# The 512-token FFN's gate and up projections: from ordinary tiles to seven block products

## The reference, cut to what matters

```
D_MODEL = 1024;  SEQ = 512;  CTX_LEN = 256;  D_FF = 2816     # 22 tiles of 128
def swiglu(h, w1, w2):
    gate, up = jnp.split(h @ w1, 2, axis=-1)
    return (jax.nn.silu(gate) * up) @ w2
def ffn_sublayer(h, m, sub, g_pre, g_post, w1, w2):
    shift, scale, gate = mods_of(m, sub)
    y = swiglu(modulate(rms_norm(h, g_pre[sub]), shift, scale), w1, w2)
    return h + MACARON_WEIGHT * gate * rms_norm(y, g_post[sub])
```

## Time and profile before

| | us |
|---|---|
| median of three timed runs | 3765.51 |
| the profiled execution | 3757.21 |
| its span, first to last instruction | 3755.4 |
| PE busy in the span | 3530.5 (94%) |
| DVE, ACT, POOL busy | 2183.8, 1434.2, 721.5 |
| 512-token FFN: first matmul of its first pair | starts at 2427.65 |
| 512-token FFN: last matmul of its output | ends at 2798.92 |

### The profile page before, as it was taken

How to read it: one execution, slowest core, us unless ns; L and a number is a source line. 1 busy time by engine, 2 the same in 40 slices (tenths; PEclk the granted TensorE clock), 3 DMA queues, 4 the chain that set the end, 5 groups by cost and what they waited for, 6 DMA issues and landing times.

```text
span 3755.4 us, 52062 instructions
## 1 busy us (share of the span) xinstructions
PE 3530.5 (94%) x19855; PEld 3030.4 (81%) x19855; DVE 2183.8 (58%) x3395; ACT 1434.2 (38%) x2510; POOL 721.5 (19%) x299
## 2 busy tenths in 40 slices
PE   6899999988999999999999898899998999899998
PEld 4899997856789999789999676788878898589656
DVE  6888875167488888788887429421226462541134
ACT  4433333157353333543334317432234423221353
POOL 1111112200211111211111220244442232034202
PEclk9999999999999999999999998999998999799899
DMA  6333332110233332433333220123332222022101
GB/s 227 107 124 123 124 120 86 62 36 1 91 118 116 121 117 97 157 109 116 113 113 119 82 70 17 46 90 100 96 95 68 62 79 68 1 73 90 62 1 56
DMA packets 94531, 333.55 MB, mean 89 GB/s; under 512 B 12272, under 2 KB 14576, under 8 KB 93424
## 3 DMA queue, kind: packets, MB, share of 16 engines
q1 hardware_dynamic: 91248, 316.28, 25.5%
q10 hardware_dynamic: 3072, 14.40, 1.0%
HBM read 322.12 MB, written 8.52 MB: 88 GB/s over the span
## 4 chain that ended last, share of the span: by engine, by line
PE 60%; issue 23%; POOL 6%; DVE 6%; ACT 3%; DMA 2%; SPq 0%; POOLq 0%; DVEq 0%; ACTq 0%
PE psum L2348 21%; PE psum L2227 14%; PE psum L2207 13%; POOL w_parts L668 6%; PE psum L2652 1%; PE psum L2668 1%; PE psum L2262 1%; PE psum L2677 1%; PE psum L2450 1%; PE psum L2121 1%; DMA mod_ring<-modw_dram 1%; PE psum L2424 1%; DVE normed L1302 1%; PE psum L2556 1%; DVE mod_products L1390 0%
## 5 line engine op out<-in xcount | busy, mean ns | idle before, releaser
L668 POOL TENSOR_TENSOR w_parts<-w_raw,w_parts 128x1024 fp32r<-128x1024 f32 x289 | 702.5, 2432 | 2929.2 <-ACT w_parts L708 2916.8
L2207 PE MATMUL psum<-h_parts,w_parts 128*128 128x264 f32 (+1 forms) x5712 | 958.2, 330 | 46.8 <-issue 11.8
L2207 PEld LDWEIGHTS psum<-h_parts,w_parts 128*128 128x128 f32 x5712 | 855.4, 191 | 144.4 <-issue 44.6
L708 ACT ACTIVATE w_parts<-w_raw 128x1024 fp32r<-128x1024 f32 x283 | 300.1, 1061 | 1123.7 <-PE psum L2207 722.5
L2227 PE MATMUL psum<-w_parts,hidden_parts 128*128 128x512 f32 x2904 | 668.3, 391 | 16.5 <-DVE hidden_parts L1262 9.6
L2227 PEld LDWEIGHTS psum<-w_parts,hidden_parts 128*128 128x128 f32 x2904 | 544.6, 188 | 135.6 <-issue 14.6
L2348 PE MATMUL psum<-h_parts,w_parts 128*128 128x384 f32 x2880 | 531.6, 336 | 16.4 <-ACT y_tok L855 14.1
L2348 PEld LDWEIGHTS psum<-h_parts,w_parts 128*128 128x128 f32 x2880 | 505.4, 189 | 20.0 <-issue 17.0
L874 ACT ACTIVATE w_parts<-psum 128x512 fp32r<-128x512 f32 x240 | 143.7, 599 | 367.9 <-PE psum L2348 147.9
L2348 PE MATMUL psum<-h_sums,w_parts 128*128 128x384 f32 x1440 | 268.9, 334 | 0.0
L2348 PEld LDWEIGHTS psum<-h_sums,w_parts 128*128 128x128 f32 x1440 | 251.3, 188 | 0.0
(11 more groups left out here) (352 smaller groups left out, 4121.1 us busy)
## 6 DMA issues: line engine op xcount, KB each, us to landing
w_raw<-wu_dram SPq DMA_DIRECT2D x295, 512.0 KB, 3.6
mod_ring<-modw_dram SPq DMA_DIRECT2D x128, 512.0 KB, 4.4
w_raw_pairs<-wg_dram SPq DMA_DIRECT2D x120, 512.0 KB, 3.7
kept_dram<-resid SPq DMA_DIRECT2D x2, 3136.0 KB, 9.9
resid<-kept_dram SPq DMA_DIRECT2D x16, 392.0 KB, 5.8
na_bias<-rpb_dram ACTq DMA_DIRECT2D x6, 896.0 KB, 4.7
four_dft<-four_dram ACTq DMA_DIRECT2D x2, 2048.0 KB, 8.1
mod_first_k<-modw_dram SPq DMA_DIRECT2D x7, 512.0 KB, 10.0
```

The lines of the kernel that those rows point to most:

```text
L668: pool.tensor_tensor(SPL[:, s % 2, 1], RAW[:, s % 2], SPL[:, s % 2, 0].bitcast(F32), ALU.subtract).then_inc(w_split, 1)
L708: act.activation(SPL[:, u % 2, 0], RAW[:, u % 2], ACT.Copy).then_inc(w_hi, 1)
L2207: ins = pe.matmul(PS[:, pair, PSO[a]:PSO[a] + z - a], w[:, wp, k], src[:, xp, k, t0 + a:t0 + z], start=k == 0 and n_ == 0, stop=k == KT - ...
```

## The change

The 512-token FFN becomes the fourth fast FFN. All code of the fast FFN that had 384 columns for half the tokens takes that number from the FFN (`half_tokens`), so the products here are 256 columns wide. The new FFN has no modulation tiles to make beside its work (`MOD_PLAN` is zero there). Its pure weight blocks get their low part from GpSimd (`run_lows`), not from DVE. The weights are stored on the host in the other order.

```
-    fast = [... if sub["kind"] == "ffn" and sub["T"] == T1]
+    fast = [... if sub["kind"] == "ffn"]
...
+            def run_lows(g):                                              # GpSimd
+                for n, (m, p) in enumerate(ORDER):
+                    if m in PURE:
+                        pool.wait_ge(block_hi, PRODUCTS * g + n + 1)
+                        pool.tensor_tensor(w_block(n, 1), raw_half(g, p, *PURE[m]), w_block(n, 0).bitcast(F32),
+                                           ALU.subtract).then_inc(block_low_pure, 1)
...
                 low_parts(start + 4, 4)
                 u = start + 8
                 for g in range(RUNS):
+                    if sub["T"] == SEQ:
+                        run_lows(RUNS * sub["fo"] + g)
                     low_parts(u, 4)
...
             def w_step(g, q):                                             # DVE
-                if q + 3 < PRODUCTS:
+                if q + 3 < PRODUCTS and (half_tokens(g // RUNS) == T1 // 2 or ORDER[q + 3][0] in SUM_BANK):
...
-                        pe.wait_ge(bank_read, yb - T1 // P + to + 1)
+                        pe.wait_ge(bank_read, yb - tiles + min(to + 1, tiles))
...
-                            ins = pe.matmul(bank(to, HT), w_block(n, wp)[:, k], moving(m, xp)[:, k], ...
+                            ins = pe.matmul(bank(to, ht), w_block(n, wp)[:, k], moving(m, xp, ht)[:, k], ...
```

More of the change, by code:

```diff
@@ L377, in build @@
     n = dict(u=0, silu=PRIME, pr=PRIME, e=PRIME, q=0, sq=PRIME, xr=PRIME, att=0, out=0, tr=0, mix=0, eh=0, ph=0, yb=6, bd=0, ys=0, yt=0)
-    fast = [idx for idx, sub in enumerate(subs) if sub["kind"] == "ffn" and sub["T"] == T1]
+    fast = [idx for idx, sub in enumerate(subs) if sub["kind"] == "ffn"]
     for idx, sub in enumerate(subs):
@@ L462, in build, with half_tokens, quarter, normed @@
     assert mod_first_of(1) == 64 and mod_first_of(2) >= MOD_TILES + MOD_FIRST and mod_first_of(3) == DEPTH * MOD_TILES
-    HT = T1 // 2
-    def quarter(i, j, x):
-        return H[:, x, 4 * i:4 * i + 4, HT * j:HT * j + HT]
-    def normed(i, j):
-        return VB[:, 4 * i:4 * i + 4, HT * j:HT * j + HT]
-    def moving(m, x):
-        return {1: quarter(0, 0, x), 2: quarter(1, 0, x), 3: quarter(1, 1, x), 4: quarter(0, 1, x),
-                5: X12[:, 0, x], 6: X12[:, 1, x], 7: X3[:, x]}[m]
+    def half_tokens(fo):
+        return subs[fast[fo]]["T"] // 2
+    def quarter(i, j, x, ht):
+        return H[:, x, 4 * i:4 * i + 4, ht * j:ht * j + ht]
+    def normed(i, j, ht):
+        return VB[:, 4 * i:4 * i + 4, ht * j:ht * j + ht]
+    def moving(m, x, ht):
+        return {1: quarter(0, 0, x, ht), 2: quarter(1, 0, x, ht), 3: quarter(1, 1, x, ht), 4: quarter(0, 1, x, ht),
+                5: X12[:, 0, x, :, 0:ht], 6: X12[:, 1, x, :, 0:ht], 7: X3[:, x, :, 0:ht]}[m]
     def w_block(n, x):
@@ L657, in _ @@
                     u += S_UNITS
-                elif idx == 1:
+                elif sub["kind"] == "mix":
                     w_loads(u, 24)
@@ L857, in fast_run @@
             def fast_run(g, u, sub):
[L859 removed]
+                base, ht = PRODUCTS * g, half_tokens(g // RUNS)
                 def block_high(n):
@@ L880, in kept @@
                         act.wait_ge(signal, free)
-                    act.activation(dst[:], bank(c_bank(p, "Q"), HT), ACT.Copy).then_inc(kept_ready, 1)
+                    act.activation(dst[:, 0:ht], bank(c_bank(p, "Q"), ht), ACT.Copy).then_inc(kept_ready, 1)
                 for q in range(-3, PRODUCTS + 4):
@@ L901, in fast_run @@
                             act.wait_ge(product_done, base + q)
-                            act.activation(TS[:, 0, HT:T1], bank(c_bank(p, "Q"), HT), ACT.Silu).then_inc(silu12_ready, 1)
+                            act.activation(TS[:, 0, ht:2 * ht], bank(c_bank(p, "Q"), ht), ACT.Silu).then_inc(silu12_ready, 1)
                     for p in range(RUN):
@@ L2322, in fast_run @@
             def fast_run(g, fo, yb):
+                ht, tiles = half_tokens(fo), subs[fast[fo]]["T"] // P
                 for n, (m, p) in enumerate(ORDER):
@@ L2347, in fast_run @@
                         for n_, (wp, xp) in enumerate(((0, 0), (0, 1), (1, 0))):
-                            ins = pe.matmul(bank(to, HT), w_block(n, wp)[:, k], moving(m, xp)[:, k], start=m in (1, 7, 2) and k == 0 and n_ == 0,
+                            ins = pe.matmul(bank(to, ht), w_block(n, wp)[:, k], moving(m, xp, ht)[:, k], start=m in (1, 7, 2) and k == 0 and n_ == 0,
                                             stop=k == 3 and n_ == 2, skip_group_check=True)
@@ L2852, in ffn @@
         gate, up = units_of(w1[:, :F_TILES * P]), units_of(w1[:, F_TILES * P:])
-        if (l, s) != (DEPTH - 1, 1):
-            us.extend([gate[0:2], up[0:2]])
-            us.extend(out_units_of(w2[f0 * P:(f0 + nf) * P], 2) for f0, nf in S_PARTS)
-            pairs.append(np.stack([gate[2:], up[2:]], 1))
-            return
-        for f0, nf in F_PARTS:
-            for f in range(f0, f0 + nf, 2):
-                us.extend([gate[f:f + 2], up[f:f + 2]])
-            us.append(out_units_of(w2[f0 * P:(f0 + nf) * P]))
+        us.extend([gate[0:2], up[0:2]])
+        us.extend(out_units_of(w2[f0 * P:(f0 + nf) * P], 2) for f0, nf in S_PARTS)
+        pairs.append(np.stack([gate[2:], up[2:]], 1))
     for l in range(DEPTH):
```

64 lines of the change are left out of this document (32 added, 32 removed).

## The result

The changed kernel takes 3770.62 us (median of 12 runs, 3764.47 to 3779.85) against 3760.98 us of the kernel before (12 runs, 3757.33 to 3771.49). The ratio is 1.0027 (95% interval 1.0019 to 1.0035): some 10 us slower. That is clear of the noise, since the interval lies above 1, but inside the 0.3% that I had called no change, and inside the forecast's own range of 3756 to 3777. From its first matmul to its last output matmul the 512-token FFN takes 381.4 us instead of 371.3, so the whole difference is in it (one profiled execution of each kernel).

What follows compares the result with a forecast made beforehand. TensorE, busy 94% of the span, was taken as the bound: 34.3 + 12.0 + 1.7 + 201.6 + 109.2 + 9.0 + 4.5 = 372.3 us against 371.3, +1.0, so a median of 3766, range 3756 to 3777.

Steps and rivals of the forecast that it cites:

- TensorE's work: Matmuls of the five runs: 0.120 us each, products lasting 1.44 us, 201.6 in all, 16.8 less than before.
- Ahead of the first run: FFN's start: 34.3 us of TensorE work, 12.0 idle (2.3 + 5.0 + 4.7) and 1.7 for a clock fall.
- GpSimd's 128x512 low part: Pure block's low part on GpSimd inside a run: taken as 1.25 us, near half of the 128x1024 one's 2.38.
- The 14th product: Inside a run: the third pair's late weights and the chain to ACT's copy make TensorE wait 0.67 us.
- The 21st product: Inside a run: by the same count of late weights, the fourth pair waits 0.95 us.
- The 7th product: Inside a run: by the same count of late weights, the second pair waits 0.2 us.
- The run's end: First output unit's low part behind GpSimd's last pure block: 0.9 us wait a run, 4.5 in all.
- The tail: FFN's end: as before; eight residual loads of 5.8 us each, covered by the last output part's 21.8 us.
- GpSimd shuts DVE out: Slower rival inside runs: GpSimd blocks DVE's two-SBUF-input instructions, DVE becomes the bound, +14 us, 3780 to 3785; chance 0.17.
- The clock inside the runs: Rival: waits inside runs pull the clock to 1.2 GHz, 1.7 us lost twice a run, +17, 3783; chance 0.04.
- the faster one: Rival: slots free earlier, GpSimd's low parts hidden, no wait inside runs or at their ends, -13.5 us, 3753; chance 0.17.

Runs made afterwards that it cites:

- e1: The changed kernel with the pure blocks' low parts moved back from GpSimd to DVE: 512-token FFN 385.9 us, ratio 1.0032 to the kernel before.
- e2: The changed kernel with GpSimd writing zeros instead of subtracting, so pure blocks' low parts are left out: 512-token FFN 371.9 us, timed once.
- e3: The changed kernel with a fourth slot for pair weights instead of three: 512-token FFN 369.6 us, ratio 0.9990 to the kernel before.
- e5: e3 with the hidden tile's high and low part one step later for a run's first three pairs: 512-token FFN 365.5 us, timed once.
- e10: e9 with the pure blocks' low parts on DVE instead of GpSimd: 512-token FFN 361.6 us, ratio 0.9958 to the kernel before.
- e9: e5 plus the first output unit's high part at step 25, its low part after the last pure block: FFN 359.8 us, ratio 0.9965 to before.
- e11: e9 on the change's three pair slots instead of four: 512-token FFN 376.5 us, ratio 0.9992 to the kernel before.

## Why the prediction held, and where it was off

It was right in its side and within its own range: no change beyond 0.3%. That 3770.6 lies so near the forecast's 3766 is in part luck. The forecast stood on a median of 3765.51 for the kernel before; over twelve runs it was 3760.98. The forecast change was +1.0 us and the measured one is 9.6, so the FFN was missed by 9 us, and "no measurable change" held because 9.6 is still under 11.3.

- *TensorE's work.* Right: products 1.44 us apart.
- *Ahead of the first run.* Right in sum, 46.1 for 48.0, by terms that were off both ways: the idle time inside the first pair was 0.8 (2.3 forecast), the wait for the hidden tile was 3.99 (5.0 forecast), the gaps behind it 0.64 + 0.44 + 1.27 = 2.35 (4.7), the clock fell behind the 3.99 and not ahead of the first product, with 1.9 us lost in 24 matmuls (1.7), and TensorE's own work is the rest, 37.0 (34.3).
- *GpSimd's 128x512 low part.* Right: 1.29 where undisturbed, 1.33 on average, for 1.25.
- *The 14th product.* The chain was right link by link, the size was not: 1.5 to 1.7 instead of 0.67. The step that failed is the time at which the slot comes free, which I had put at 2.1 behind the 7th product; it came 1.5 later. Two things were left out of it. In the list of DVE instructions with both inputs in SBUF I counted "two products, one split" and left out the two sums that read two halves of a pair slot: the sum for product 5, put at 0.61, took 0.93 on average and up to 1.58. And ACT makes the high part of a sum block first, 0.6. e1 shows that the wait stays, at 1.04 to 1.78, when GpSimd holds nothing ahead of it; e2, without any low parts of pure blocks, leaves about half of it; a fourth slot takes all of it (e3).
- *The 21st product.* 0.63 to 0.72 in four runs and 2.03 in the last, for 0.95. The reason given, the same chain of late weights, is wrong for the four: a fourth slot leaves them at 0.63 (e3), and the place of the hidden tile's high part on ACT makes them (e5). It holds for the last, where the load took 4.82 us.
- *The 24th product.* Not forecast: 0.46, about 0.7 with its hand-over. In the change it is the split that meets GpSimd (e2, e5); with the low parts on DVE, those take its place (e1).
- *The 7th product.* 0.48 in the first run and none in the others, for 0.2.
- *The run's end.* Right: 0.73 idle for 0.9, released by GpSimd.
- *The tail.* Right: 3.00 ahead of the transposition, as before.
- In sum a run of after loses 4.5 us (second run) and not 2.7; with the first run's and the last run's extra waits that is the 10.7 by which the five runs miss.
- *The rivals.* That GpSimd shuts DVE out is there, but not with the end that was given to it (whose sum, 22 in place of 9, makes +13 and not +14). DVE did not become the bound, since DVE with all low parts still keeps up (e10); it was late by 0.3 to 0.9 at single places in the runs, and TensorE paid for those that its next wait hung on. The Trainium skill's rule in "SBUF — State Buffer", section "Who interferes with whom", held in all its parts that these runs touch: instructions of DVE with two inputs in SBUF are held by GpSimd's reads (1.58 against 0.70), those with one input there are not (L1542 at 700 ns), and GpSimd's writes don't hold them (e2, 698 ns). The clock inside the runs stayed at 1.00, so that rival is out, and so is the faster one in this form; e9 shows the 11 us that it would have needed.

Open is how much of the late slots in the kernel after is the lock. e1 takes the lock away and puts as much work on DVE in its place, and e2 makes GpSimd shorter at the same time, so no run removes the lock alone. The same holds for e11's 1.8 ahead of the 21st product: late weights make it, but GpSimd holds sums there too (1075 ns on average), and that may be part of why they are late.

## What to carry to other kernels

When a change makes each piece of TensorE's work shorter, divide the load chain of a buffer (release, issue, landing, first reader) by the new piece: three slots left most pairs without a gap at 2.08 us and not at 1.44, and the waits that came of it took back what the saved arithmetic gave (11.8 us with e3's fourth slot). Before work goes to GpSimd, list every DVE instruction that reads two tiles in SBUF, the sums of weights too, and place GpSimd's reads where none that TensorE waits for stands beside them. An engine's busy share didn't tell either: what counted was which instruction stood ahead of the one copy that TensorE waited for.
